# Loading and splitting the first two weight pieces of a stage ahead of its opening

## The chip, the cores and the metric

The kernel runs on one core of one Trainium2 chip. The metric is the device time of one execution in microseconds (us). A core has a matrix engine (TensorE, PE in the profile; its weight loads are PEld), a vector engine (VectorE, DVE), an activation engine (ScalarE, ACT), a general engine (GpSimd, POOL) and a queue engine that issues most transfers (SyncE, SP; SPq in the rows). Engines meet at semaphores only. A block of the program ends in a barrier that all engines must reach.

## The reference, cut to what matters

Five parts follow one another on 512 rows of 1024 numbers, all in float32:

```
h = x
h = layer_norm(alpha*h + window_attention(h))        # layer 0
h = layer_norm(alpha*h + hier_moe(h))                # expert stage 0: 32 experts, each token in 2
h = layer_norm(alpha*h + latent_attention(h))        # layer 1: c = h @ b_w_down, ...
h = layer_norm(alpha*h + hier_moe(h))                # expert stage 1
for l in range(2):                                   # second block
    p = rms_norm(h, norm_mix_pre[l]) @ w_in[l]       # 1024 x 3072, 12 slices of 256 columns
    h = h + rms_norm(mixers(p) @ w_out[l]);  h = h + rms_norm(conv_ffn(rms_norm(h)))
```

`hier_moe` ends in a weighted sum: each token adds the outputs of its two experts, each times its routing weight.

## The kernel before, in words

Rows are worked on in four tiles of 128 rows (`NT` = 4, tile t). The residual stream is `resid`. Products that need float32 accuracy are made from split operands: a value is stored as a high part (rounded, made on ScalarE by `high`) and a low part (value minus high part), and `split_matmul` (L242 to L244) multiplies high by high, high by low and low by high. A weight arrives in pieces of 1 MB, as 128 partitions x 2048 numbers. A piece is loaded into one of two places of `raw`, then `high` (L1646, L2452) and `low` (L1796, L2692) write its parts.

**Expert stage** (`experts`). For each of 32 blocks of 64 slots the weights (6 MB) are streamed in through SP's queue, three sets deep. PE multiplies (L1219, L1237), POOL scatters the results of a block by an indirect DMA into `y_dram` (`r_y`, L1191). SP issues its last weight load long before the last block is done. The stage ends when the last scatter has landed. The tile `hT`, 16 KB in each partition, is not used while this stage runs.

**Opening** of the part behind it (`latent_layer` behind stage 0, `second_block` behind stage 1). It makes the sum of the residual and the experts' rows, a layer norm, in the second block also an RMS norm, a transposition, and a split, tile by tile:

- SP loads `rows[t]` (L499, 1 MB each, from `r_y`), the norm's gain and shift (L428, L429, 0.5 MB each), and the first two weight pieces (L1386, L2047).
- PE: `own` (L512) multiplies `resid` of all four tiles by the identity, into two PSUM banks a tile. `add(t)` (L520) adds the two weighted rows of tile t, and waits for `rows[t]`. After the norm `turn_x(t)` (L1443) or `turn(opening, t)` (L2109) transposes the tile back into the same banks.
- DVE: for tile t `stats` (L446, L448) on PSUM, `centre` (L467), `finish` (L474), and `split_low(t)` (L1787, L2712). In the second block `finish(opening, t)` (L2708) scales by the RMS norm in between.
- ACT: the square root and its companions, `split_high(t)` (L1628, L2474), `high(0)`, `high(1)`.
- POOL makes the low parts of weight pieces 0 and 1 (L1436, L2095). All later low parts are made by DVE.

After the opening PE starts the first product with the first half of the columns (tiles 0 and 1, 256 columns) and does the second half (tiles 2 and 3) when these are there. In the latent layer this is `down_tile(m, columns)` with six output tiles m: before, m = 0 and 1 are done in halves, m = 2 to 5 whole. Each half of a tile is 24 matmuls of 256 columns, a whole one 24 of 512. In the second block it is `in_halves`: four output tiles q of weight pieces 0 and 1, first halves with `turn` calls in between, then the four second halves.

In the latent layer, SP waits until two output tiles are complete (`sp.wait_ge(down, 2)`), since the rotary tables (L1406) and the next weight pieces of `b_w_uq` come after that. ACT makes the high part of that piece (L1644) before it copies output tile 0 out of PSUM (L1651) and squares it (L1655), and PE's `add_squares(0)` (L1459) needs the square.

Between expert stage 1 and the second block stands `sweep`, a block of its own with a barrier on either side, in which POOL, DVE and ACT clear semaphores and SP issues the first loads.

## Time and profile before

| | |
|---|---|
| median of 3 runs | 2841.07 us (2838.81 to 2842.73) |
| profiled execution, device time | 2843.17 us |
| its span in the trace | 2841.4 us |
| TensorE matmul busy | 2533.8 us, 89% |
| VectorE busy | 1078.5 us, 38% |
| ScalarE busy | 776.1 us, 27% |
| GpSimd busy | 179.0 us, 6% |
| opening of the latent layer | from 755.2 us on |
| opening of the second block | from 1570.2 us on |

Times in the rows are microseconds from the start of the span. In a timeline row the first number is the start, the second the time from the start of the first to the end of the last of the x instructions of the row, and in brackets stands how long the engine sat idle before it and what it waited for. The trace shows a float32 matmul of 512 columns as two instructions: `own` and `add` have 16 and 32 rows where the program has 8 and 16 matmuls. PEclk is the granted TensorE clock as a share of full speed: 1.00 is 2.4 GHz and 0.50 is 1.2 GHz.

### The profile page before, as it was taken

To read this page: it belongs to the slowest core of one execution; us is meant where nothing else is said; L and a number is where in the kernel's file an instruction comes from. 1 tells how busy PE (TensorE), PEld (TensorE's weight loads), DVE (VectorE), ACT (ScalarE), POOL (GpSimd) and SP (SyncE) were. 2 spreads that over 40 slices of the span, in tenths; PEclk is the share of its full clock that TensorE was granted. 3 is DMA by queue.
4 is the path that set the end of the run, shared out by engine and by line. 5 is a ranking of instruction groups with operands and counts; after the bars stand their busy time and mean duration, and the time that the engine had idled before them with its cause. 6 is when DMAs were issued, how large, how long until landed. Compare 5 with 4: busy or idle time off the path is not lost. (4 is left out here: it accounts for less than half of the span.)

```text
span 2841.4 us, 36857 instructions
## 1 busy us (share of the span) xinstructions
PE 2533.8 (89%) x14546; PEld 1870.4 (66%) x14546; DVE 1078.5 (38%) x1597; ACT 776.1 (27%) x1234; POOL 179.0 (6%) x284
## 2 busy tenths in 40 slices
PE   8796998887788978997887699999999999999998
PEld 7574555544366665654454487788878876888887
DVE  3653111001244551110000465655551566655632
ACT  3430101000135420100000343543431453544331
POOL 0000111111100001111111100000000000000000
PEclk9996999999998978999999799999999999999999
DMA  5228999999712068999998421313232222232331
GB/s 155 60 79 317 409 407 405 408 409 406 258 71 75 9 260 348 405 406 409 406 413 327 146 97 60 119 60 104 89 120 102 82 71 78 79 100 89 104 119 52
DMA packets 174815, 576.39 MB, mean 203 GB/s; under 512 B 20497, under 2 KB 104017, under 8 KB 125043
## 3 DMA queue, kind: packets, MB, share of 16 engines
q1 hardware_dynamic: 164146, 558.07, 51.7%
q0 software_dynamic: 10560, 16.81, 1.8%
q8 instruction: 77, 1.26, 0.2%
q14 instruction: 32, 0.25, 0.0%
HBM read 569.56 MB, written 23.07 MB: 209 GB/s over the span
## 5 line engine op out<-in xcount | busy, mean ns | idle before, releaser
L1219 PE MATMUL ps<-first_weights,moe_xsT 128*64 128x256 f32 x2688 | 312.3, 381 | 49.9 <-DMA first_weights<-in_moe_w_up 33.1
L242 PE MATMUL ps<-l_h_hi,l_w_hi 128*128 128x512 f32 x896 | 353.0, 394 | 0.0
L244 PE MATMUL ps<-l_h_hi,l_w_lo 128*128 128x512 f32 x896 | 348.8, 389 | 0.0
L243 PE MATMUL ps<-l_h_lo,l_w_hi 128*128 128x512 f32 x896 | 348.8, 389 | 0.0
L1275 DVE TENSOR_TENSOR moe_hid<-moe_silu,ps 128x256 f32<-128x256 f32 x64 | 27.0, 422 | 796.3 <-PE ps L1219 796.3
L1219 PEld LDWEIGHTS ps<-first_weights,moe_xsT 128*64 128x64 f32 x2688 | 223.7, 137 | 148.3 <-issue 98.8
L2692 DVE TENSOR_TENSOR l_w_lo<-l_raw,l_w_hi 128x2048 fp32r<-128x2048 f32 x76 | 174.0, 2292 | 290.7 <-ACT l_w_hi L2452 290.7
L1256 ACT ACTIVATE moe_ys<-ps 128x512 f32<-128x512 f32 x64 | 38.2, 597 | 688.6 <-PE ps L1237 688.6
L1237 PE MATMUL ps<-first_weights,moe_hidT 128*64 128x512 f32 x672 | 177.2, 675 | 38.6 <-DVE moe_hidT L1277 38.6
L2452 ACT ACTIVATE l_w_hi<-l_raw 128x2048 fp32r<-128x2048 f32 x76 | 145.2, 1914 | 187.2 <-PE ps L244 176.3
L1219 PE MATMUL ps<-first_ring,moe_xsT 128*64 128x256 f32 x1408 | 168.5, 388 | 30.7 <-DMA first_ring<-in_moe_w_up 17.1
L242 PEld LDWEIGHTS ps<-l_h_hi,l_w_hi 128*128 128x128 f32 x896 | 168.2, 188 | 37.4 <-issue 2.9
L243 PEld LDWEIGHTS ps<-l_h_lo,l_w_hi 128*128 128x128 f32 x896 | 168.3, 188 | 35.5 <-issue 1.4
L244 PEld LDWEIGHTS ps<-l_h_hi,l_w_lo 128*128 128x128 f32 x896 | 168.2, 188 | 35.5
L1219 PEld LDWEIGHTS ps<-first_ring,moe_xsT 128*64 128x64 f32 x1408 | 119.0, 140 | 84.2 <-issue 58.9
L1237 PEld LDWEIGHTS ps<-first_weights,moe_hidT 128*64 128x64 f32 x672 | 60.0, 152 | 126.8 <-issue 126.8
L1237 PE MATMUL ps<-first_ring,moe_hidT 128*64 128x512 f32 x352 | 87.2, 639 | 20.1 <-DVE moe_hidT L1277 20.1
L1203 PEld LDWEIGHTS ps<-cst,moe_xs 64*128 64x128 f32 x528 | 68.8, 215 | 43.3 <-issue 24.6
L1203 PE MATMUL ps<-cst,moe_xs 64*128 64x64 f32 x528 | 77.9, 289 | 18.1 <-DMA moe_xs<-r_x,moe_take 18.1
L1191 POOL DMA_INDIRECT r_y<-moe_ys,moe_put x64 | 65.6, 1025 | 295.0 <-ACT moe_ys L1256 295.0
L2735 DVE SCALAR_TENSOR_TENSOR l_gate<-l_glu,l_par,l_gate 128x512 f32<-128x512 f32 x120 | 81.0, 744 | 0.1
L242 PE MATMUL ps<-l_w_hi,l_act_hi 128*128 128x512 f32 x192 | 77.0, 401 | 3.6 <-DVE l_conv L2866 3.6
(549 smaller groups left out, 4294.4 us busy)
## 6 DMA issues: line engine op xcount, KB each, us to landing
first_weights<-in_moe_w_up SPq DMA_DIRECT2D x84, 1024.0 KB
first_weights<-in_moe_w_down SPq DMA_DIRECT2D x84, 1024.0 KB
first_weights<-in_moe_w_gate SPq DMA_DIRECT2D x84, 1024.0 KB
first_ring<-in_moe_w_gate SPq DMA_DIRECT2D x44, 1024.0 KB
first_ring<-in_moe_w_up SPq DMA_DIRECT2D x44, 1024.0 KB
first_ring<-in_moe_w_down SPq DMA_DIRECT2D x44, 1024.0 KB
l_raw<-in_ffn_up SPq DMA_DIRECT2D x44, 1024.0 KB, 5.1
l_raw<-in_w_in SPq DMA_DIRECT2D x24, 1024.0 KB, 5.3
```

The lines of the kernel that those rows point to most:

```text
L242: pe.matmul(out, stationary[0], moving[0], start=first, stop=False)
L243: pe.matmul(out, stationary[0], moving[1], start=False, stop=False)
L244: return pe.matmul(out, stationary[1], moving[0], start=False, stop=last)
L1191: pool.indirect_dma_start(out=r.y_dram, out_offset=bass.IndirectOffsetOnAxis(ap=put[:, 0:1], axis=0), in_=ys[:, :], in_offset=None, bounds ...
L1203: ins = pe.transpose(k.ps[:, 0, j * SLOTS:(j + 1) * SLOTS], row_of_tile[:, j // 4, j % 4, :], k.cst[0:SLOTS, C_ID:C_ID + SLOTS])
L1219: ins = pe.matmul(k.ps[64 * h:64 * h + 64, 2 + m, 0:256], xsT[:, j, :], weights.gate_up[s][m][:, j, 256 * h:256 * h + 256], start=j == 0, ...
L1237: ins = pe.matmul(k.ps[64 * h:64 * h + 64, 4, :], hidT[:, j % 2, 64 * (j // 2):64 * (j // 2) + 64], weights.down[s][:, j, 512 * h:512 * h ...
L1256: act.activation(ys[:, :], k.ps[:, 4, :], ACT.Copy).then_inc(ys_kept, 1)
L1275: dve.tensor_tensor(hid[:, :], silu[:, :], k.ps[:, 3, 0:256], ALU.mult).then_inc(hid_kept, 1)
L2452: act.activation(ring[n][0], raw[:, m % 2, :], ACT.Copy).then_inc(hi_made, 1)
L2692: dve.tensor_tensor(lo, raw[:, m % 2, :], hi.bitcast(F32), ALU.subtract).then_inc(lo_made, 1)
L2735: ins = dve.scalar_tensor_tensor(acc, glu[:, i, c:c + SEQ], par[:, l, 2, 2 * c + i:2 * c + i + 1], acc, ALU.mult, ALU.add)
```

## The change

At the end of each expert stage SP issues the first two weight pieces of the part that follows, into `hT` (`k.early`). The opening's ACT and DVE split them first, ahead of the norm's work; POOL no longer does. `own` is called tile by tile between the `add` calls. In the latent layer the first halves of four output tiles, not two, are done before tiles 2 and 3 of the rows are needed. In the second block's `sweep` SP issues only two `rows` loads, PE does `own(0)` there, and the gains, `rows[2]` and `rows[3]` are issued behind the barrier. The order of `split_low`, `stats` and `finish` changes.

```diff
 def sweep(self, loads, products):
+            @block.tensor
+            def _(pe):
+                products(pe)
...
-    def own(self, k, pe):
-        for t in range(NT):
-            for half in range(2):
+    def own(self, k, pe, t):
+        for half in range(2):
...
 def experts(k, layer, r, weights, early):
                 weights.load(sp, layer, LAST_SET, e, free(LAST_SET, q + TURNS))
+            for n in range(2):
+                src, j = early(n)
+                sp.dma_start(k.early[:, n, :].rearrange("p (j c) -> p j c", j=j), src).then_inc(r.early_in, 16)
...
 def latent_layer, SP
-                if p >= 2:
+                if p >= 4:
                     sp.wait_ge(lo_made, done_of(p - 2))
...
-            load(0)
             cl.load(sp, 2)
             cl.load(sp, 3)
-            load(1)
 latent_layer, POOL
-            for p in range(2):
-                pool.wait_ge(hi_made, p + 1)
-                pool.tensor_tensor(whole(p, 1), raw[:, p, :], whole(p, 0).bitcast(F32), ALU.subtract).then_inc(lo_made, 1)
 latent_layer, PE
-            for m in range(2):
-                down_tile(m, slice(2 * P, SEQ)).then_inc(down, 1)
-            for m in range(2, 6):
-                down_tile(m, slice(0, SEQ)).then_inc(down, 1)
-                if m < 5:
+            for m in range(6):
+                down_tile(m, second if m < 4 else slice(0, SEQ)).then_inc(down, 1)
+                if 2 <= m < 5:
                     add_squares(m - 2)
 latent_layer, ACT
-            act.preload_act_table_set("natural_log_exp_and_others")
             cl.diagonals(k, act)
+            high(0)
+            high(1)
+            act.preload_act_table_set("natural_log_exp_and_others")
 latent_layer, DVE
+            low(0)
+            low(1)
             stats(0)
...
             split_low(0)
+            split_low(1)
             stats(2)
             cm.centre(k, dve, 2, tile_banks(2))
-            split_low(1)
...
 second_block, before its block
     def first_loads(sp):
         cl.load(sp, 0)
-        cm.load_gains(k, sp, DEPTH - 1, 1)
-        for t in range(1, NT):
-            cl.load(sp, t)
-    k.sweep(first_loads)
+        cl.load(sp, 1)
+    k.sweep(first_loads, lambda pe: cl.own(k, pe, 0))
 second_block, SP
-            load(0, 0)
-            load(0, 1)
+            cm.load_gains(k, sp, DEPTH - 1, 1)
+            cl.load(sp, 2)
+            cl.load(sp, 3)
 second_block, PE, the turns after first halves 0 to 3
-                in_halves(..., *([((), (2,), (), (3,))] if l == 0 else []))
+                in_halves(..., *([((), (2,), (3,), ())] if l == 0 else []))
```

PE at the opening of the latent layer. The number behind `lat_rows` is a buffer, in the order of tiles 0 to 3. Before:

```order
L512 MATMUL ps<-resid,cst 128x512 x8
L520 MATMUL ps<-lat_rows_3336,lat_diag 128x512 x4
L520 MATMUL ps<-lat_rows_3337,lat_diag 128x512 x4
...
L520 MATMUL ps<-lat_rows_3338,lat_diag 128x512 x4
...
L520 MATMUL ps<-lat_rows_3339,lat_diag 128x512 x4
```

After:

```order
L519 MATMUL ps<-resid,cst 128x512 x4
L527 MATMUL ps<-lat_rows_3338,lat_diag 128x512 x4
L519 MATMUL ps<-resid,cst 128x512 x2
L527 MATMUL ps<-lat_rows_3339,lat_diag 128x512 x4
L1457 MATMUL ps<-cst,resid 128x128 x8
L519 MATMUL ps<-resid,cst 128x512 x2
L527 MATMUL ps<-lat_rows_3340,lat_diag 128x512 x4
L1457 MATMUL ps<-cst,resid 128x128 x8
L527 MATMUL ps<-lat_rows_3341,lat_diag 128x512 x4
```

Four of the eight identity matmuls now stand behind the first `add`, two of them behind the first transposition.

DVE at the opening of the second block, up to the low part of tile 1 (`l_h_lo`, second row). Before:

```order
L446 BN_STATS l_cstats<-ps 128x6 x2
L448 BN_AGGR l_cmv<-l_cstats 128x2
L467 SCALAR_TENSOR_TENSOR resid<-ps,l_cmv,l_cgain 128x1024
L2697 RECIPROCAL l_rs<-l_sd 128x1
L2708 SCALAR_TENSOR_TENSOR l_end_xn_7165<-resid,l_rs,l_end_gain_7162 128x1024
L2884 RECIPROCAL l_crs<-l_clnv 128x1
L474 SCALAR_TENSOR_TENSOR resid<-resid,l_crs,l_cshift 128x1024
L2712 TENSOR_TENSOR l_h_lo<-ps,l_h_hi 128x8x128
L446 BN_STATS l_cstats<-ps 128x6 x2
L448 BN_AGGR l_cmv<-l_cstats 128x2
L467 SCALAR_TENSOR_TENSOR resid<-ps,l_cmv,l_cgain 128x1024
```

After:

```order
L2721 TENSOR_TENSOR l_first_lo<-first_hT,l_first_hi 128x2048 x2
L454 BN_STATS l_cstats<-ps 128x6 x2
L456 BN_AGGR l_cmv<-l_cstats 128x2
...
L482 SCALAR_TENSOR_TENSOR resid<-resid,l_crs,l_cshift 128x1024
L454 BN_STATS l_cstats<-ps 128x6 x2
L456 BN_AGGR l_cmv<-l_cstats 128x2
L475 SCALAR_TENSOR_TENSOR resid<-ps,l_cmv,l_cgain 128x1024
L2741 TENSOR_TENSOR l_h_lo<-ps,l_h_hi 128x8x128
L2726 RECIPROCAL l_rs<-l_sd 128x1
L2737 SCALAR_TENSOR_TENSOR l_end_xn_7215<-resid,l_rs,l_end_gain_7211 128x1024
```

Two low parts of 2048 numbers now stand ahead of the first statistics, and the statistics and centring of tile 2 ahead of the low part of tile 0.

SP around the end of expert stage 1: the two pieces are now the last issues of the stage (`first_hT`), and their old place is gone:

```order
L1175 DMA first_hT<-in_w_in 128x8x256 x2
...
L507 DMA l_rows_7217<-r_y 128x2x1024
L507 DMA l_rows_7218<-r_y 128x2x1024
...
L507 DMA l_rows_7219<-r_y 128x2x1024
L507 DMA l_rows_7220<-r_y 128x2x1024
```

## Rows read from the trace of the kernel before

**Rows 1.** The page, costliest groups: splitting one piece, low and high part.

```profile
L2692 DVE TENSOR_TENSOR l_w_lo<-l_raw,l_w_hi 128x2048 fp32r<-128x2048 f32 x76 | 174.0, 2292 | 290.7 <-ACT l_w_hi L2452 290.7
...
L2452 ACT ACTIVATE l_w_hi<-l_raw 128x2048 fp32r<-128x2048 f32 x76 | 145.2, 1914 | 187.2 <-PE ps L244 176.3
```

**Rows 2.** Busy time by stretch: last blocks of stage 0, openings.

```profile
core 0: us, PE busy (x) PEld busy (x) DVE busy (x) ACT busy (x) POOL busy (x), PEclk, DMA share, GB/s
...
734.00:736.00 2.00, 1.78 (x16) 1.26 (x16) 0.00 (x0) 0.11 (x1) 0.00 (x0) 1.00 0.54 224
...
744.00:746.00 2.00, 1.08 (x6) 0.17 (x2) 0.00 (x0) 0.60 (x1) 0.00 (x0) 1.00 0.00 0
...
1597.00:1608.00 11.00, 1.16 (x9) 0.80 (x7) 8.95 (x8) 4.34 (x6) 4.49 (x1) 0.76 0.00 0
...
1631.00:1637.00 6.00, 5.62 (x27) 5.62 (x28) 4.82 (x3) 2.67 (x2) 0.00 (x0) 0.52 0.01 3
1637.00:1646.00 9.00, 9.00 (x77) 8.85 (x75) 0.00 (x0) 0.09 (x1) 0.25 (x2) 1.00 0.00 0
```

**Rows 3.** Timeline of the latent layer's opening, up to its first products.

```profile
755.21 9.28 PE L512 MATMUL ps<-resid,cst 128*128 128x512 f32 x16 [10.13 <-PEq L1148]
...
767.96 1.30 DVE L446 BATCH_NORM_STATS2 lat_cstats<-ps 128x6 f32<-128x512 f32 x2 [26.38 <-PE ps L520]
...
771.01 1.28 DVE L474 SCALAR_TENSOR_TENSOR resid<-resid,lat_crs,lat_cshift 128x1024 f32<-128x1024 f32 x1
...
782.84 0.39 PE L242 MATMUL ps<-lat_x_hi,lat_d_hi 128*128 128x256 f32 x1 [0.50 <-DVE lat_x_lo L1787]
...
793.90 0.58 PE L242 MATMUL ps<-lat_x_hi,lat_d_hi 128*128 128x256 f32 x1 [2.37 <-DVE lat_x_lo L1787]
```

**Rows 4.** Timeline of the latent layer behind its opening.

```profile
801.35 0.34 SPq L1406 DMA_DIRECT2D lat_tables<-in_k_ropeb  x1
...
806.93 1.57 ACT L1644 ACTIVATE lat_u_hi<-lat_raw 128x1024 fp32r<-128x1024 f32 x2 [11.72 <-DMA lat_raw<-in_b_w_uq]
...
809.53 0.70 PE L1459 MATMUL ps<-lat_sq,cst 128*128 128x512 f32 x1 [2.74 <-ACT lat_sq L1655]
...
832.60 0.50 PE L242 MATMUL ps<-lat_c_q_hi,lat_u_hi 128*128 128x512 f32 x1 [1.22 <-DVE lat_u_lo L1794]
```

**Rows 5.** Timeline of the second block's opening.

```profile
1574.12 2.45 ACT L505 ACTIVATE l_diag<-cst,r_weight 128x128 f32<-128x128 f32 x8 [13.29 <-PEq L189]
...
1583.39 13.90 PE L520 MATMUL ps<-l_rows,l_diag 128*128 128x512 f32 x32
...
1587.02 1.30 DVE L446 BATCH_NORM_STATS2 l_cstats<-ps 128x6 f32<-128x512 f32 x2 [30.39 <-PE ps L520]
...
1594.62 1.29 DVE L2708 SCALAR_TENSOR_TENSOR l_end_xn<-resid,l_rs,l_end_gain 128x1024 f32<-128x1024 f32 x1
...
1602.53 4.49 POOL L2095 TENSOR_TENSOR l_first_lo<-l_raw,l_first_hi 128x2048 fp32r<-128x2048 f32 x1 [28.29 <-ACT l_first_hi L2452]
...
1603.35 4.76 DVE L2708 SCALAR_TENSOR_TENSOR l_end_xn<-resid,l_rs,l_end_gain 128x1024 f32<-128x1024 f32 x1
...
1608.16 1.97 PE L2109 MATMUL ps<-cst,l_end_xn 128*128 128x128 f32 x8 [10.01 <-DVE l_end_xn L2708]
...
1612.50 0.58 PE L242 MATMUL ps<-l_h_hi,l_first_hi 128*128 128x256 f32 x1 [2.37 <-DVE l_h_lo L2712]
...
1646.30 0.50 PE L242 MATMUL ps<-l_h_hi,l_w_hi 128*128 128x512 f32 x1
```

**Rows 6.** DMA issues and time to landing: tiles 0 and 1, scatters.

```profile
lat_rows<-r_y SPq DMA_DIRECT2D x1, 1024.0 KB, 5.2
...
lat_rows<-r_y SPq DMA_DIRECT2D x1, 1024.0 KB, 9.5
...
DMA to landing us min/median/max: 2.6/6.6/13.8
...
746.66 1.02 POOL L1191 DMA_INDIRECT r_y<-moe_ys,moe_put  x1 [4.11 <-ACT moe_ys L1256]
```

More of the change, by code:

```diff
@@ L183, in clear_stale, with early, sweep @@
                 eng.sem_clear(s)
-    def sweep(self, loads):
+    @property
+    def early(self):
+        return self.hT[:, :, :].rearrange("p (n a) s -> p n (a s)", n=2)
+    def sweep(self, loads, products):
         sems = [s for st in self.stale for s in st.sems]
@@ L1127, in for_each_block, with experts @@
         body(LAST_SET, q + TURNS, q + (EXPERTS - 1))
-def experts(k, layer, r, weights):
+def experts(k, layer, r, weights, early):
     st = Stage(k.nc, f"moe{layer}")
@@ L1555, in out_part @@
                     ins.then_inc(am.out_made, 1)
-            cl.own(k, pe)
+            first, second = slice(0, 2 * P), slice(2 * P, SEQ)
+            cl.own(k, pe, 0)
+            cl.own(k, pe, 1)
             cl.add(k, pe, 0)
+            cl.own(k, pe, 2)
             cl.add(k, pe, 1)
             turn_x(0)
+            cl.own(k, pe, 3)
             cl.add(k, pe, 2)
@@ L1639, in high @@
                     act.wait_ge(up, len(kinds))
-                act.wait_ge(loaded[p % 2], 16 * (p // 2 + 1))
-                src = raw[:, p % 2, 0:size(p)]
+                if p < 2:
+                    act.wait_ge(before.early_in, 32)
+                else:
+                    act.wait_ge(loaded[p % 2], 16 * (p // 2))
+                src = source(p)
                 if split(p):
@@ L1790, in low @@
                 dve.wait_ge(hi_made, done_of(p))
-                src = raw[:, p % 2, 0:size(p)]
+                src = source(p)
                 if split(p):
@@ L2024, in second_block @@
     tile_cols = lambda x, t: x[:, :, t * P:(t + 1) * P]
+    piece = lambda m: k.early[:, m, :] if m < 2 else raw[:, m % 2, :]
     unit_bank = lambda u: u if u < 8 else u % 2
@@ L2091, in _ @@
             pool.wait_ge(cleared, 2)
-            for n in range(2):
-                hi, lo = ring[n]
-                pool.wait_ge(hi_made, n + 1)
-                pool.tensor_tensor(lo, raw[:, n, :], hi.bitcast(F32), ALU.subtract).then_inc(lo_made, 1)
             for l in range(DEPTH):
@@ L2403, in turn_parameters @@
                     ins.then_inc(par_turned, 1)
-            cl.own(k, pe)
-            for t in range(NT):
-                cl.add(k, pe, t)
+            cl.own(k, pe, 1)
+            cl.add(k, pe, 0)
+            cl.own(k, pe, 2)
+            cl.add(k, pe, 1)
+            cl.own(k, pe, 3)
+            cl.add(k, pe, 2)
+            cl.add(k, pe, 3)
             turn(opening, 0)
@@ L2450, in high @@
                 m = PIECES * l + n
-                act.wait_ge(loaded[m % 2], 16 * (m // 2 + 1))
-                act.activation(ring[n][0], raw[:, m % 2, :], ACT.Copy).then_inc(hi_made, 1)
+                if m < 2:
+                    act.wait_ge(before.early_in, 32)
+                else:
+                    act.wait_ge(loaded[m % 2], 16 * (m // 2))
+                act.activation(ring[n][0], piece(m), ACT.Copy).then_inc(hi_made, 1)
             def root(g, n, t):
@@ L2653, in _ @@
             cl.diagonals(k, act)
+            high(0, 0)
+            high(0, 1)
             act.wait_ge(cleared, 2)
@@ L2659, in _ @@
             finish(opening, 1, None)
-            high(0, 0)
             deviation(2)
             split_high(opening, 1)
-            high(0, 1)
             finish(opening, 2, None)
             deviation(3)
+            finish(opening, 3, None)
             split_high(opening, 2)
-            finish(opening, 3, None)
             split_high(opening, 3)
@@ L2885, in normed @@
                 cm.finish(k, dve, t)
+            low(0, 0)
+            low(0, 1)
             stats(0)
@@ L2892, in _ @@
             normed(1)
+            stats(2)
             split_low(opening, 0)
-            stats(2)
             finish(opening, 1)
+            normed(2)
             split_low(opening, 1)
-            normed(2)
             stats(3)
             finish(opening, 2)
-            split_low(opening, 2)
             normed(3)
             finish(opening, 3)
+            split_low(opening, 2)
             split_low(opening, 3)
-            dve.wait_ge(lo_made, 2)
             for l in range(DEPTH):
```

38 lines of the change are left out of this document (22 added, 16 removed).

## The prediction

> **What bounds the kernel now.** I read first the busy time by stretch. At full clock PE is busy in every microsecond once a stage runs: 77 matmuls of 256 columns in 9.00 us between 1637 and 1646 [rows 2]. The two openings are where it is not: between 1597 and 1608 PE is busy 1.16 us of 11, and no transfer runs (DMA share 0.00), so DVE (8.95 us) holds it up. Then the timelines, to see which wait ends last. In the latent layer's opening PE spends 9.28 us on `own` alone, adds, and starts its first product at 782.84; it stops again 2.37 us before 793.90, for the low part of tile 3 [rows 3]. In the second block it waits 10.01 us for the scaled tile 1, then 2.37 us, and starts at 1612.50 [rows 5]. What PE loses in an opening the kernel loses, since all behind it hangs on PE's first products. The expert stages are bound by their 1 MB loads, but these are over before the end: the DMA share is 0.54 at 734 to 736 and 0.00 at 744 to 746 [rows 2], and the last scatter is issued at 746.66 [rows 6].
>
> **What is moved, and the price of each part.**
>
> *The early loads* (2 MB a stage) stand behind the last weights in SP's queue. Rows of tile 0 (1 MB) land 5.2 us after issue, tile 1 9.5 us after an issue 1.4 us later, with 1 MB of gains between: 2 MB in some 5.7 us, 2.85 us a MB. Two pieces so take 5.7 us. The last weights run out between 736 and 744; the pieces then end near 745, before the scatter of 746.66. I take 0. Bounds: a scatter takes 2.6 us at best, 6.6 in the median and 13.8 at most [rows 6]; so 0 to 11.2 us a stage, and the value nearest to the stretch with share 0.00 is 0. A gain in the stage itself is excluded, since its own loads are not fewer.
>
> *The split on ACT and DVE*: 2 high parts of 1.91 us, 2 low parts of 2.29 us [rows 1]. ACT starts them after its eight diagonals (2.45 us), DVE ends 2 x 2.29 us after the first high part: 2.45 + 1.91 + 4.58 = 8.9 us after the barrier.
>
> *POOL's two low parts go.* POOL took 4.49 us from 1602.53; the DVE instruction that started at 1603.35 took 4.76 us, where the same instruction took 1.29 us at 1594.62 [rows 5]: it ended 1.1 us after POOL did. These 3.5 us lie inside PE's wait of 10.01 us and go with it.
>
> *Latent layer.* Barrier at 755.2. PE: four instructions for each tile of `own`, eight for each `add`, at 0.43 us each (13.90 us / 32, [rows 5]); the first five come at half clock (9.28 = 5 x 0.85 + 11 x 0.44 and some, [rows 3]). So `own` of tiles 0 and 1 ends at 760.8; rows 0 landed at 760.4. `add(0)` ends at 764.3, and DVE's low parts at 755.2 + 8.9 = 764.1: stats of tile 0 start at 764.4 instead of 767.96. Finish ended 4.33 us after the start of stats (771.01 + 1.28 - 767.96); now at 768.7. Rows 1 land at 766.1 (756.6 + 9.5), just as `own(2)` ends; `add(1)` to 769.6, turn 0 to 770.5 (0.9 each), `own(3)` to 772.3, `add(2)` to 775.8, turn 1 to 776.9, `add(3)` to 780.4. Tile 1: stats from 769.7, finished 774.0, high part after the turn to 778, low part 1.2 us later, 779.2, so hidden. The first product starts at 780.4, 2.4 us earlier. Then PE has four first halves of 2.9 us (24 x 0.12) and two turns, 13.5 us, to 794.0; tile 2 is finished at 783.4 (stats 779.2, + 4.2), just when turn 2 comes; tile 3 at 788.8, its low part at 793.5. The wait of 2.37 us and the half clock behind it go. Output tiles 0 and 1 complete at 794.0 + 2 x 2.9 = 799.8; before it was 801.2, when SP issued the tables (801.35, [rows 4]): 1.4 us earlier.
>
> What is late next is the piece of `b_w_uq`, as before. It landed 5.6 us behind 801.35, at 806.93, and only then did ACT come to the square, which PE got at 809.53, 8.3 us after output tile 1 [rows 4]. That distance stays: now 808.1. But PE has only a half of output tile 2 left to do in it (2.9 us) and waits 5.4 us instead of 2.74. Behind it output tile 3 is a half instead of a whole: 2.9 us instead of the 5.5 that tile 2 took as a whole (from 801.2 to 809.53 - 2.74 = 806.8), 2.6 less. The rest up to 832.60 (squares, root, low parts, PE idle 1.22) hangs on the third square and stays. Gain: 1.4 + 2.6 = **4.0 us**. Half clock behind the wait costs the same as before: it was there too behind 2.74 us.
>
> *Second block.* The barrier of `sweep` stays at 1574.1: SP has three issues less, but `own(0)` in it takes 4 x 0.85 = 3.4 us from 1570.2, to 1573.6. Then `own(1)` 2.0 us; the diagonals are ready at 1576.6, and `add(0)` ends at 1580.1. The remaining two `own` (1.75 each) and three `add` (3.5 each) end at 1594.2; before, 1583.39 + 13.90 = 1597.3. Transfers keep ahead: 2 MB of rows from 1570.2, then gains 1 MB by about 1580.5, rows 2 and 3 by 1583.3 and 1586.2. DVE: low parts until 1574.1 + 8.9 = 1583.0, then stats of tile 0: 1583.1 instead of 1587.02, so the two low parts cost 3 us against `add(0)` and yet leave 3.9 us. The scaled tile 0 came 8.9 us behind the start of stats (1594.62 + 1.29), tile 1's norm 10.3 us; now 1592.0 and 1593.4. Stats and centre of tile 2 to 1596.3 (2.9 us). PE turns tile 0 at 1594.2 to 1595.2, ACT's high part to 1596.3, DVE's low part to 1597.6; ACT squares tile 1 (1.05 + 0.5) to 1597.8; DVE scales tile 1 to 1599.4 instead of 1608.1. Turn 1 to 1600.5, high part (behind ACT's next root) to 1601.6, low part to 1602.9. The first product starts at **1603.0 instead of 1612.5**: 9.5 us.
>
> Then two first halves with half clock at the start (2.9 x 2 + 1.7) to 1610.5; tile 2 was scaled at 1607.3, so turn 2 does not wait; a first half to 1614.3, tile 3 scaled at 1612.0, turn 3, the last first half to 1618.1; tile 3's low part is there at 1617.5. Four second halves (11.5) and the parameters (1.0): 1630.6 where PE was at 1646.30. Of the **15.7 us**, 9.5 are the earlier start, 1.1 + 2.37 two waits that go, 2.4 the half clock behind them (27 matmuls in 5.62 us at clock 0.52, against 0.117 us each, [rows 2]), 0.3 rounding. What follows (tables, pieces 4 on) is issued on PE's progress and moves along.
>
> Sum: 4.0 + 15.7 = 19.7 us. The profiled execution took 2843.17 us, 2.1 above the median; 2843.2 - 19.7 = 2823.5 there, and **2821.4** against the median. Its own range is 2817 to 2826: either opening may be wrong by 2 to 3 us, above all the order of ACT's short waits, and the barrier of `sweep` by 1 us each way.
>
> **Rivals.**
>
> *The latent layer gains nothing.* SP's wait for two complete output tiles comes as late as before: two more first halves (5.8 us) now stand ahead of them, and I leave only 1.4 us of play. If tile 3's low part or turn 2 is late by that, the piece of `b_w_uq` is late and the half tile moved forward is only a longer wait at the square. Then 0 to 1 us there and 15.7 in the second block: 2825. For it: PE's wait at 809.53 exists. Against: PE's chain up to 799.8 has no wait in my table.
>
> *PE stays at half clock in the second block.* It idles 4.3 us behind turn 0 and 2.5 behind turn 1, and the turns are 1 us of work. Before, with idle of 10.0 and 2.37 us, it came back 3.8 us behind 1612.50, and I count the same. If all four first halves go at 0.208 instead of 0.117 us, 96 x 0.09 - 1.7 = 7 us are lost: 2828.5. Against: that start was no better prepared.
>
> *The pieces come late* (the change doesn't do what it says): they would land only behind the barrier, ahead of the rows. Rows then come 5.7 us later in both openings, less the 5.7 us of pieces that no longer stand between: high(0) on both engines waits, and each opening loses about 5: 2832. Against: from 744 to the barrier at 755.2 only the last scatter moves.
>
> *Slower.* The last scatter of each stage, which alone ends it, meets the early pieces. Each would land after up to 13.8 us instead of 2.6 [rows 6]: 2 x 11.2 = 22.4, against 19.7, so 2844. It decides from 9.9 us a stage on. The Trainium skill ("DMA: Bandwidth & Descriptors", section on queues, rings and completion order) has each DMA engine alternate between the queues that have work, whole packets at a time. By this rule a scatter that meets the pieces is held up and not just queued behind them; the rows agree (6.6 us in the median, most of them beside streaming weights, against 2.6 at best).
>
> From the rows alone the milder case of it is 6.6 - 2.6 = 4 us a stage, were the pieces still running at 746.66. Against: share 0.00 at 744 to 746 leaves them room.
>
> **Chances.** Forecast 0.60; latent layer without gain 0.15; half clock 0.08; a scatter held up for 4 us a stage 0.06 (2821.4 + 8 = 2829.4); late pieces 0.04; slower 0.03; 0.04 for more gain than I see (2812 to 2817: the barrier of `sweep` earlier, tile 1 earlier on ACT). The range 2815 to 2830 leaves out about 0.15. No change (within 0.2%, 5.7 us, about what a measurement of this kernel can tell) needs a loss of 14 us against the sum: 0.03. Faster 0.95, slower 0.02.
>
> **What would show it.** In the profile of the changed kernel: the first 256-column product of the latent layer 25.2 us behind the barrier (before 27.6), a wait at the square of about 5 us, PE's first product on `c_q` 73.4 us behind it (before 77.4). In the second block the first product 28.9 us behind `sweep`'s barrier instead of 38.4, no wait between its halves, the 512-column products from 56.5 us on instead of 72.2. The DVE scaling of tile 1 takes 1.3 us. The span of an expert stage is unchanged, and no weight piece is waited for by `high(0)`. I am wrong if the last scatters take over 3 us, if `high(0)` waits for DMA, or if time appears between the openings' ends and the end of the kernel.

## The result, and the profile after

| | median of 4 runs | lowest, highest | ratio to before, 95% interval |
|---|---|---|---|
| before | 2841.28 us | 2838.81, 2842.73 | |
| changed | 2825.61 us | 2823.35, 2828.97 | 0.9946 [0.9931, 0.9962] |

The change gives 15.7 us by the medians. The forecast was 2821.4 us, or 19.7 us less. The measured time lies in its range, 4.2 us above the point. The profiled execution took 2828.97 us with a span of 2827.1: the slowest of the four, so its stages are set beside a second profile of the same kernel below.

The page of the changed kernel, busy times:

```profile
span 2827.1 us, 36949 instructions
...
PE 2532.8 (90%) x14594; PEld 1869.7 (66%) x14594; DVE 1079.9 (38%) x1601; ACT 776.0 (27%) x1234; POOL 159.5 (6%) x280
```

PE does the same work (2533.8 us before). POOL lost 19.5 us. What changed is when PE may start.

The timeline of the latent layer's opening (start, us, engine and line, operation, in brackets the idle time before it and its releaser). The barrier is at 756.6:

```profile
756.66 6.48 PE L519 MATMUL ps<-resid,cst 128*128 128x512 f32 x8 [10.12 <-PEq L1156]
...
760.90 4.49 DVE L1817 TENSOR_TENSOR lat_d_lo<-first_hT,lat_d_hi 128x2048 fp32r<-128x2048 f32 x2 [19.57 <-ACT lat_d_hi L1667]
...
766.61 1.30 DVE L454 BATCH_NORM_STATS2 lat_cstats<-ps 128x6 f32<-128x512 f32 x2 [1.21 <-PE ps L527]
...
781.49 0.68 PE L250 MATMUL ps<-lat_x_hi,lat_d_hi 128*128 128x256 f32 x1
...
801.53 0.34 SPq L1423 DMA_DIRECT2D lat_tables<-in_k_ropeb  x1
...
807.25 1.57 ACT L1665 ACTIVATE lat_u_hi<-lat_raw 128x1024 fp32r<-128x1024 f32 x2 [10.70 <-DMA lat_raw<-in_b_w_uq]
...
809.85 2.07 PE L1473 MATMUL ps<-lat_sq,cst 128*128 128x512 f32 x2 [5.48 <-ACT lat_sq L1676]
...
830.43 0.50 PE L250 MATMUL ps<-lat_c_q_hi,lat_u_hi 128*128 128x512 f32 x1 [1.22 <-DVE lat_u_lo L1815]
```

Against [rows 3, 4], counted from the barrier: statistics after 10.0 us (before 12.75), the first product after 24.9 (27.6; forecast 25.2), the first product on `c_q` after 73.8 (77.4; forecast 73.4). The wait of 2.37 us for the low part of tile 3 is gone. The wait at the square doubled from 2.74 to 5.48 us, as forecast (5.4).

The second block's opening, barrier of `sweep` at 1575.4:

```profile
1575.39 2.44 ACT L513 ACTIVATE l_diag<-cst,r_weight 128x128 f32<-128x128 f32 x8 [13.10 <-PEq L193]
...
1579.67 4.49 DVE L2721 TENSOR_TENSOR l_first_lo<-first_hT,l_first_hi 128x2048 fp32r<-128x2048 f32 x2 [21.57 <-ACT l_first_hi L2481]
...
1584.08 1.29 DVE L454 BATCH_NORM_STATS2 l_cstats<-ps 128x6 f32<-128x512 f32 x2
...
1598.85 1.28 DVE L2737 SCALAR_TENSOR_TENSOR l_end_xn<-resid,l_rs,l_end_gain 128x1024 f32<-128x1024 f32 x1
...
1600.19 1.97 PE L2131 MATMUL ps<-cst,l_end_xn 128*128 128x128 f32 x8 [3.99 <-DVE l_end_xn L2737]
...
1604.53 0.58 PE L250 MATMUL ps<-l_h_hi,l_first_hi 128*128 128x256 f32 x1 [2.37 <-DVE l_h_lo L2741]
...
1632.19 0.50 PE L250 MATMUL ps<-l_h_hi,l_w_hi 128*128 128x512 f32 x1
```

These answer to [rows 5]. The diagonals start at 1575.4 and not at 1574.1, since the stage before ended 1.5 us later; from the barrier on the first product comes after 29.1 us (before 38.4; forecast 28.9) and the 512-column products after 56.8 (72.2; forecast 56.5). The wait of 10.01 us for the scaled tile 1 is now 3.99. DVE's scaling, held up for 3.5 us by POOL, takes 1.28 us again.

Busy time by stretch (the columns are those of [rows 2]): PE in the stretch where it did 1.16 us of 11 before, and in the last 15 us before the 512-column products, where it no longer stops.

```profile
1597.00:1608.00 11.00, 5.44 (x24) 5.04 (x25) 8.79 (x13) 4.42 (x10) 0.00 (x0) 0.57 0.09 30
...
1617.00:1632.00 15.00, 15.00 (x127) 14.75 (x125) 5.72 (x3) 4.83 (x5) 0.25 (x2) 1.00 0.01 1
```

To see where the time went, I cut each profile at the same instructions. *Stage*: first to last scatter of an expert stage. The *tail* is from the last scatter's issue to SP's first issue behind the barrier. *Opening 1*: from there to the first product on `c_q`. *Latent, late*: from SP's issue of the first piece of `b_w_o` to its issue of the gain for the layer norm at the end of the latent layer. *Opening 2*: from SP's first issue in `sweep` to the first 512-column product. The table leaves out three stretches. The one before stage 0 and the one from the first product on `c_q` to the first piece of `b_w_o` differ by under 0.7 us in these five profiles; the one from the end of the latent layer to the first scatter of stage 1 is 189.0 to 191.7 us long. All in us, one profiled execution each:

| kernel | stage 0 | tail | opening 1 | latent, late | stage 1 | tail | opening 2 | opening 2 to end |
|---|---|---|---|---|---|---|---|---|
| before | 468.9 | 8.5 | 77.4 | 45.3 | 469.0 | 8.5 | 76.1 | 1195.1 |
| changed | 470.7 | 8.5 | 73.8 | 46.4 | 470.9 | 8.5 | 60.5 | 1194.9 |
| changed, second profile | 467.9 | 8.5 | 73.6 | 46.4 | 471.7 | 8.5 | 60.1 | 1194.6 |
| opening 1 alone | 467.4 | 8.5 | 74.0 | 46.4 | 471.3 | 8.4 | 76.4 | 1195.0 |
| opening 2 alone | 469.1 | 8.5 | 77.8 | 45.4 | 472.4 | 8.5 | 60.1 | 1192.0 |

Openings gain 3.6 and 15.6 us in the first profile of the changed kernel, 3.8 and 16.0 in the second: 19.2 to 19.8, and 19.7 were forecast. 1.1 us are given back in the late part of the latent layer, in the three profiles here with the new latent opening. The rest of the 4 us lies in expert stages and in the stretch ahead of stage 1, which both vary by 2 us and more between profiles of one kernel. So the questions for the experiments were: does opening 1 deliver, are the scatters held up, and what in the change is it that pays.

### The profile page after: what moved, and what is told of

Read it like the earlier page. It is cut to its first block and busy times, and to the rows that moved or that the text cites. A ratio compares the mean times of both kernels' runs of the same rounds, so it can differ in the third digit from the quotient of the medians.

```text
span 2827.1 us, 36949 instructions
## 1 busy us (share of the span) xinstructions
PE 2532.8 (90%) x14594; PEld 1869.7 (66%) x14594; DVE 1079.9 (38%) x1601; ACT 776.0 (27%) x1234; POOL 159.5 (6%) x280
## 5 line engine op out<-in xcount | busy, mean ns | idle before, releaser
L1248 PE MATMUL ps<-first_weights,moe_hidT 128*64 128x512 f32 x672 | 177.2, 675 | 38.6 <-DVE moe_hidT L1288 38.6
L1248 PEld LDWEIGHTS ps<-first_weights,moe_hidT 128*64 128x64 f32 x672 | 60.1, 152 | 126.8 <-issue 126.8
L1248 PE MATMUL ps<-first_ring,moe_hidT 128*64 128x512 f32 x352 | 88.8, 650 | 20.1 <-DVE moe_hidT L1288 20.1
L1214 PE MATMUL ps<-cst,moe_xs 64*128 64x64 f32 x528 | 77.9, 289 | 19.2 <-DMA moe_xs<-r_x,moe_take 19.2
L1264 ACT ACTIVATE moe_silu<-ps 128x256 f32<-128x256 f32 x64 | 24.5, 383 | 203.2 <-PE ps L1230 203.2
## 6 DMA issues: line engine op xcount, KB each, us to landing
first_weights<-in_moe_w_up SPq DMA_DIRECT2D x84, 1024.0 KB, 29.1
first_weights<-in_moe_w_down SPq DMA_DIRECT2D x84, 1024.0 KB, 28.9
```

The source lines that it names most:

```text
L1214: ins = pe.transpose(k.ps[:, 0, j * SLOTS:(j + 1) * SLOTS], row_of_tile[:, j // 4, j % 4, :], k.cst[0:SLOTS, C_ID:C_ID + SLOTS])
L1248: ins = pe.matmul(k.ps[64 * h:64 * h + 64, 4, :], hidT[:, j % 2, 64 * (j // 2):64 * (j // 2) + 64], weights.down[s][:, j, 512 * h:512 * h ...
```

## Experiments

Opening 1 is that of the latent layer, opening 2 that of the second block. Theory A is the forecast's: both openings gain what was worked out, and nothing is lost outside them. Theory B: the early loads lengthen the stages. Theory C: the latent layer's gain is handed back behind it.

### The same kernel again, opening 1 alone, opening 2 alone

The changed kernel was measured again, beside two kernels that each undo one half of the change. Opening 1 alone:

```diff
     # second block: pieces 0 and 1 from raw again, low parts by POOL, order as before
-            for n in range(2):
+            for n in range(2 if early else 0):
                 src, j = early(n)
-            cl.own(k, pe, 1)
-            cl.add(k, pe, 0)
...
+            for t in range(NT):
+                cl.own(k, pe, t)
+            for t in range(NT):
+                cl.add(k, pe, t)
```

Opening 2 alone undoes the same in the latent layer, with `experts(k, 0, routes[0], weights, None)` and two halves of output tiles instead of four.

> The changed kernel again, for a closer ratio and as the yardstick of the runs beside it. In the profiled execution the two openings gave 3.7 and 15.6 us, while both expert stages were 1.8 us longer and 1.8 us were lost in the latent layer behind its opening. Theory A (chance): the stages and the latent layer wobble by about 2 us from execution to execution, so here these three places come out otherwise: the stages within 1 us of before, the median 15 to 19 us below before. Theory B (contention): the two early pieces hold up the last weights and the last scatter, 1.8 us in each stage in every execution; median 15.5 below. Theory C (given back): what the latent layer's opening gains is lost again before the next expert stage, whatever the run: again 0.3 to 1 us left there.

> Only expert stage 0 loads pieces early, and only the latent layer's opening is changed; stage 1 and the second block are as before. Theory A: 3 to 4 us faster than before. Theory B: 3.7 - 1.8, 2 us faster. Theory C: 0 to 1 us faster.

> Only expert stage 1 loads pieces early, and only the second block's opening is changed. Theory A: 15 to 16 us faster. Theory B: 13.8 us faster, and stage 1 is 1.8 us longer. Theory C says the same as A here. If this alone gives what the whole change gives (15.5), the latent layer's part was worth nothing.

| kernel | median | ratio, interval | gain against 2842.91 |
|---|---|---|---|
| changed | 2826.32 us | 0.9940 [0.9928, 0.9953] | 16.6 |
| opening 1 alone | 2841.68 us | 0.9994 [0.9985, 1.0003] | 1.2, not told from 0 |
| opening 2 alone | 2827.48 us | 0.9943 [0.9930, 0.9956] | 15.4 |

Within the error the second opening is the whole measured gain: 15.4 us where 15.7 were forecast for it. The first one is worth 1.2 us, with an interval from a gain of 4.3 to a loss of 0.9, where 4.0 were forecast. Its own stretch is shorter by 3.4 us in the profile of that very kernel (74.0 against 77.4), so Theory A holds locally. Theory C holds for a part of it: 1.1 us are lost again at one place. PE waits there for the same ScalarE work for the same time. The kernel before, the row and its stretch:

```profile
881.57 0.71 PE L1504 MATMUL ps<-lat_k,lat_q 64*128 64x128 f32 x8 [2.53 <-ACT lat_probs L1691]
...
880.50:887.00 6.50, 4.87 (x30) 3.70 (x30) 1.91 (x7) 2.14 (x9) 0.00 (x0) 0.74 0.00 0
```

The changed kernel in its second profile:

```profile
876.54 1.23 PE L1518 MATMUL ps<-lat_k,lat_q 64*128 64x128 f32 x8 [2.52 <-ACT lat_probs L1712]
...
875.50:882.00 6.50, 5.46 (x30) 4.36 (x30) 1.91 (x7) 1.58 (x7) 0.00 (x0) 0.57 0.00 0
```

The wait is 2.53 and 2.52 us. But behind it the granted clock is 0.74 before and 0.57 now, and the same eight matmuls take 0.71 and 1.23 us. That is a loss the sum had no row for.

It doesn't come with every kernel that has the new opening. The kernel below in which every piece is loaded twice has the same opening, and its late part takes 45.3 us, as before:

```profile
878.03 1.03 PE L1521 MATMUL ps<-lat_k,lat_q 64*128 64x128 f32 x8 [2.53 <-ACT lat_probs L1715]
```

Over all twelve profiles of this document the wait is 2.52 or 2.53 us, and the late part is 45.3 to 45.4 us in four of them and 46.3 to 46.4 us in eight. That the moment at which PE arrives decides between the two is a guess; no run shifts that moment alone.

### The early loads held back until the last weights have landed

```diff
+            wait_then_tick(sp, loaded[LAST_SET][5], n * 16 + TURNS * 16, tick_sp)
-            for n in range(2):
-                src, j = early(n)
+            for p in range(2):
+                src, j = early(p)
...
```

SP waits for the last weights to land before it issues the two pieces.

> The changed kernel, but SP issues the two early pieces only when the last weights of the stage have landed (it waits for the semaphore of the last load), near 740 and 1552. The pieces can then delay no weights, at most the last scatter. Theory A: within 1 us of the changed kernel. Theory B: if the weights were held up, up to 3.6 us faster than it; if it is the scatter, the same or slower, with a last scatter that takes over 3 us to land.

Measured: 2828.95 us, 0.9942 [0.9929, 0.9954], from five executions; a sixth that took 8806 us is left out. That is 2.6 us more than the changed kernel. Its timeline, stage 0 and stage 1:

```profile
743.56 1.02 SPq L1176 DMA_DIRECT2D first_hT<-in_b_w_down  x2
...
749.71 1.02 POOL L1203 DMA_INDIRECT r_y<-moe_ys,moe_put  x1 [5.81 <-ACT moe_ys L1268]
...
759.41 0.37 SPq L507 DMA_DIRECT2D lat_rows<-r_y  x1
...
1562.66 1.02 POOL L1203 DMA_INDIRECT r_y<-moe_ys,moe_put  x1 [4.11 <-ACT moe_ys L1268]
...
1572.98 0.88 SPq L507 DMA_DIRECT2D l_rows<-r_y  x2
```

Nothing moved in the stages: 471.2 and 469.0 us without the pieces beside the weights, against 470.7 and 470.9, 467.9 and 471.7 with them. So Theory B is not borne out in stage 0. Over all twelve profiles stage 0 takes 469.1 us in the median with pieces behind the weights, and 468.9, 469.1 and 471.2 without. Stage 1 takes 471.2 us in the median of nine with them (469.8 to 472.4), and 469.0, 469.0 and 471.3 without: too few to tell. What did move is the tail. The pieces now run beside the last scatter, and from it to the barrier it is 9.7 and 10.3 us instead of 8.5. The trace shows it at the scatter itself: it lands 3.9 and 4.2 us after its issue, against 2.6 or 2.7 us in both stages of the kernel before and of the changed kernel. This is the mechanism of the slower rival, at a price of 1.2 and 1.8 us, not 9.9; together they are about the 2.6 us between the medians.

In the changed kernel SP issues the pieces some 28 us and more ahead of the last scatter (they queue behind the weights), and they are nearly through when it comes. Its timeline and the busy time by stretch in stage 0:

```profile
717.86 20.28 SPq L1175 DMA_DIRECT2D first_hT<-in_b_w_down  x2
...
748.11 1.02 POOL L1202 DMA_INDIRECT r_y<-moe_ys,moe_put  x1 [5.82 <-ACT moe_ys L1267]
```

```profile
740.00:742.00 2.00, 1.09 (x6) 0.48 (x7) 1.02 (x2) 0.00 (x0) 1.06 (x2) 0.96 1.06 360
742.00:744.00 2.00, 2.00 (x7) 0.61 (x5) 0.00 (x0) 0.00 (x0) 0.29 (x2) 0.50 0.50 163
744.00:746.00 2.00, 2.00 (x10) 0.76 (x6) 0.00 (x0) 0.00 (x0) 0.00 (x0) 0.69 0.12 39
```

The last column but one is the DMA share: it falls to 0.12 behind 744. The second piece lands at 747.5, 0.6 us ahead of the scatter's issue at 748.11, where the forecast had it near 745. In stage 1 of the same profile it lands at 1564.3, 1.1 us behind the scatter's issue at 1563.18, and the scatter still takes 2.7 us, with only a small rest left (DMA share 0.07 from 1562 to 1563). So the loads cost nothing, but with little to spare.

The clock of 0.50 and 0.69 beside it can't be put down to the change. In this stage the products of the last block (L1248) took 5.35 us instead of 3.65, and the scatter waited 5.82 us instead of 4.11. The second profile has these 1.7 us at the end of stage 1 and not of stage 0, the kernel with opening 1 alone has them in stage 1, where it loads nothing early, and in the kernel before 9 of the 32 blocks of each stage show such a wait, though neither last one does.

### Every piece loaded twice

```diff
+            for turn in range(2):
+                if turn:
+                    sp.wait_ge(r.early_in, 32)
                 for n in range(2):
```

and the waits for `early_in` in both openings doubled: 4 MB a stage instead of 2.

> The changed kernel, but when the two early pieces have landed SP loads both into the same place once more: 4 MB instead of 2 MB behind the last weights, the second 2 MB from about 746 to 753 and 1559 to 1566, over the last scatter. Where the scatter is held up by running pieces the stage's tail (issue of the last scatter to the barrier, 8.5 us with the pieces done, 9.7 and 10.3 us with the pieces issued late) is 10 to 13 us in both stages: 3 to 9 us more than the changed kernel in all. If a scatter isn't held up, the tail stays at 8.5 us.

Measured: 2829.04 us, 0.9955 [0.9938, 0.9971], where two kernels measured with it took 2824.61 us (`own` in one go) and 2825.50 us (two halves). Stage 1 in its timeline:

```profile
1559.82 0.99 SPq L1178 DMA_DIRECT2D first_hT<-in_w_in  x2
...
1560.27 1.02 POOL L1205 DMA_INDIRECT r_y<-moe_ys,moe_put  x1 [5.81 <-ACT moe_ys L1270]
...
1573.46 0.88 SPq L507 DMA_DIRECT2D l_rows<-r_y  x2
```

The second turn of pieces is issued from 1559.82 on, right with the scatter of 1560.27, and the barrier comes 13.2 us behind it instead of 8.5. The scatter itself lands after 7.1 us instead of 2.7. In stage 0 the second turn is issued at 746.96, 1.1 us behind the scatter of 745.84, which then lands after 3.0 us, and the tail is 8.8 us. So two pieces that meet the last scatter cost up to 4.7 us there. The Trainium skill ("DMA: Bandwidth & Descriptors", section on queues, rings and completion order) has each DMA engine alternate between the queues that have work, a packet at a time. By this rule the scatter is slowed beside the pieces, not queued behind all of them. The trace agrees, without proving the rule: both pieces were issued ahead of the scatter, at 1559.82 and 1560.23, and it landed at 1567.4, while the second piece landed at 1568.3.

### POOL makes the low parts again

```diff
+            for n in range(2):
+                hi, lo = ring[n]
+                pool.wait_ge(hi_made, n + 1)
+                pool.tensor_tensor(lo, piece(n), hi.bitcast(F32), ALU.subtract).then_inc(lo_made, 1)
...
-            low(0, 0)
-            low(0, 1)
             stats(0)
```

The same in the latent layer, where ACT also waits for POOL's two low parts before it splits tile 0: loads early, order new, but DVE no longer makes the two low parts.

> The changed kernel, but GpSimd makes the low parts of pieces 0 and 1 again, from the early pieces, in both openings; ScalarE makes the high parts early, as changed. If the gain is in the earlier order alone, this is no worse than the changed kernel, and 2.9 us a opening better, since VectorE starts its statistics at once (the add of tile 0 ends 1.2 and 2.9 us before VectorE's two low parts do). If what mattered was to keep GpSimd away from VectorE, VectorE's instructions with two SBUF inputs are held again for up to 4.5 us each while GpSimd works (about 762 to 771 and 1580 to 1589), and the openings are 2 to 5 us longer than changed. I expect the latter in the second block, by 2 us, since finish and scale of tile 0 fall into that stretch.

Measured: 2824.85 us, 0.9936 [0.9922, 0.9951]; openings 73.9 and 60.6 us. I had expected a loss of about 2 us, and there is none. Its timeline of the second opening:

```profile
1580.34 9.01 POOL L2124 TENSOR_TENSOR l_first_lo<-first_hT,l_first_hi 128x2048 fp32r<-128x2048 f32 x2 [4.28 <-ACT l_first_hi L2488]
...
1582.40 1.29 DVE L454 BATCH_NORM_STATS2 l_cstats<-ps 128x6 f32<-128x512 f32 x2 [24.06 <-PE ps L527]
...
1586.08 4.35 DVE L482 SCALAR_TENSOR_TENSOR resid<-resid,l_crs,l_cshift 128x1024 f32<-128x1024 f32 x1
```

DVE is again held up: an instruction of 1.28 us takes 4.35, and ends just behind POOL's (1589.35). But its statistics start at 1582.40, as soon as PE is ready, and not at 1584.08 behind its own low parts; counted from SP's first issue that is 1.9 us earlier. So 3.1 us are lost and 1.9 us won, and the opening takes 60.6 us, as it does in the changed kernel (60.5 and 60.1). The Trainium skill ("SBUF — State Buffer", section on the two separate sides) has a VectorE instruction with two inputs in SBUF and a GpSimd instruction that reads SBUF exclude each other for a whole instruction; this row and the 4.76 us of [rows 5] agree. So in the new order it doesn't matter for the time who makes the low parts. POOL's were ready at 1589.35, behind the first statistics, and that was early enough for PE's first product, which came at 1605.17. Before, the first low part was made from 1602.53 on, in the middle of the norm's work. The pieces were there long before that: they landed at 1589.7 and 1592.6, and ACT took them up at 1600.49 and 1611.09. So with the old load place a new order on ACT alone might also have gained something; no run tries it.

### `own` in one go

```diff
             cl.own(k, pe, 1)
-            cl.add(k, pe, 0)
             cl.own(k, pe, 2)
+            cl.own(k, pe, 3)
+            cl.add(k, pe, 0)
             cl.add(k, pe, 1)
```

in both openings, all four `own` ahead of the first `add`.

> The changed kernel, but PE does the identity matmuls of all tiles ahead of the first add again (in the second block tile 0 in the sweep, the other three ahead of the first add). They are the same instructions, so PE's adds end at the same time; the add of tile 0 ends 3.5 us later in the latent layer (768.0 after the barrier times of 756.6: 1.7 + 1.7 us of identity matmuls ahead), VectorE starts its statistics as much later, and the first product comes 1 to 3 us later there. In the second block the low parts hide it: the statistics of tile 0 start at 1584.1 against an add that would end at 1585.0, so under 1.5 us. If the interleaving does nothing, both openings are within 0.5 us of the changed kernel.

Measured: 2824.61 us, 0.9934 [0.9917, 0.9951]; openings 74.2 and 60.8 us, 0.2 to 0.7 us longer each than in the two profiles of the changed kernel. The statistics start later (766.98 in the latent layer, 12.2 us behind the barrier instead of 10.0):

```profile
754.78 8.73 PE L519 MATMUL ps<-resid,cst 128*128 128x512 f32 x16 [10.13 <-PEq L1156]
...
766.98 1.29 DVE L454 BATCH_NORM_STATS2 lat_cstats<-ps 128x6 f32<-128x512 f32 x2 [3.46 <-PE ps L527]
```

Of these 2.2 us nothing reaches the first product, which comes 24.9 us behind the barrier in both kernels; the 1 to 3 us expected there did not come. And 74.2 us lies within what the other profiles with four halves show (72.8 to 74.4). Tile by tile `own` alone is worth nothing that can be told from 0.

### Two halves instead of four in the latent layer

```diff
             down_tile(1, first)
-            down_tile(2, first)
             turn_x(3)
-            down_tile(3, first)
...
-                down_tile(m, second if m < 4 else slice(0, SEQ)).then_inc(down, 1)
+                down_tile(m, second if m < 2 else slice(0, SEQ)).then_inc(down, 1)
```

> The changed kernel, but in the latent layer only output tiles 0 and 1 are done in halves, as before. By the forecast's chain PE then runs out of halves about 5 us before tile 3's low part is there, stops and comes back at half clock, the two complete output tiles come 0.5 to 1.5 us later, and output tile 3 is a whole one behind the square: the products on c_q start 3 to 4 us later than changed, which is nearly the whole 3.7 us that this opening gained. If the gain there came from the early pieces and the earlier start alone, it is within 1 us of the changed kernel.

Measured: 2825.50 us, 0.9936 [0.9919, 0.9953], no different from the changed kernel. Opening 1 is 74.5 us, 0.7 to 0.9 longer, and the late part is 45.3 us again, 1.1 shorter: nearly the same sum. One profile can't tie that late part to the two halves: with four halves and every piece loaded twice it is 74.4 and 45.3 us. Its timeline:

```profile
788.05 1.09 PE L1457 MATMUL ps<-cst,resid 128*128 128x128 f32 x8 [1.13 <-DVE resid L482]
...
791.51 0.58 PE L250 MATMUL ps<-lat_x_hi,lat_d_hi 128*128 128x256 f32 x1 [2.37 <-DVE lat_x_lo L1806]
...
799.98 0.34 SPq L1423 DMA_DIRECT2D lat_tables<-in_k_ropeb  x1
...
808.02 1.13 PE L1473 MATMUL ps<-lat_sq,cst 128*128 128x512 f32 x2 [2.60 <-ACT lat_sq L1674]
...
814.48 1.02 PE L1473 MATMUL ps<-lat_sq,cst 128*128 128x512 f32 x2
```

PE stops again for 2.37 us at 791.51, but SP's tables are issued 45.0 us behind the barrier, and in the changed kernel 44.9: the two more first halves bring the first two output tiles no earlier. From the first square to the next it takes 6.46 us here, 8.01 before (809.53 to 817.54) and 5.54 in the changed kernel (809.85 to 815.39), where half a tile less of work lies between. The waits ahead were 2.60, 2.74 and 5.48 us. The stretch behind each, first before, then with two halves, then the changed kernel:

```profile
809.50:814.50 5.00, 4.97 (x13) 3.65 (x14) 0.86 (x2) 1.55 (x3) 0.00 (x0) 0.66 0.59 210
```

```profile
808.00:813.00 5.00, 4.98 (x20) 3.79 (x21) 0.86 (x2) 1.54 (x3) 0.00 (x0) 1.00 0.58 210
```

```profile
809.80:813.80 4.00, 3.95 (x13) 2.92 (x14) 0.89 (x2) 1.57 (x3) 0.00 (x0) 0.53 0.48 162
```

With two halves the clock stayed full. The same work at the same kind of wait went 1.55 us faster than before, and that pays for most of what the four halves save. In the seven profiles with four halves and the wait of 5.2 to 5.5 us, the step from square to square takes 5.35 to 6.58 us, at a clock of 0.50 to 0.68 over the first 5 us.

### Weight pieces of `b_w_uq` ahead of SP's wait, and a second step

The square's wait of 5.48 us is for the piece of `b_w_uq`, which SP issues only behind two complete output tiles. Two pieces are moved ahead of that wait:

```diff
             load(3)
+            load(4)
+            load(5)
             sp.wait_ge(down, 2)
             sp.dma_start(tables[:, :, :], a["k_ropeb"]).then_inc(tab_in, 16)
-            for p in range(4, O + 4):
+            for p in range(6, O + 4):
```

> The changed kernel, and in the latent layer SP issues the second and third piece of b_w_uq before it waits for two complete output tiles, not behind. The wait of 5.5 us at the first square hangs on the second of these pieces. If that wait is what took the worth of the moved half tile, it goes: ScalarE comes to the square about 2.5 us behind output tile 0, and the latent layer's products on c_q start 5 to 7 us earlier (5.5 us wait and the half clock behind it); median 4 to 6 us below the changed kernel. If something else is as late (the low parts of b_w_uq on VectorE, GpSimd, the root), 0 to 2 us.

Measured: 2815.48 us, 0.9908 [0.9893, 0.9922]. Its timeline:

```profile
769.29 26.31 SPq L1405 DMA_DIRECT2D lat_raw<-in_b_w_uq  x3
...
798.36 0.33 SPq L1425 DMA_DIRECT2D lat_tables<-in_k_ropeb  x1
...
801.04 1.02 PE L1475 MATMUL ps<-lat_sq,cst 128*128 128x512 f32 x2
...
819.82 0.50 PE L250 MATMUL ps<-lat_c_q_hi,lat_u_hi 128*128 128x512 f32 x1 [1.22 <-DVE lat_u_lo L1817]
```

The wait at the square is gone. Opening 1 takes 66.3 us instead of 73.6 to 73.8, so 7.2 to 7.5 us less, where 5 to 7 were expected for it; the stretch from there to the issue of `b_w_o` is 23.9 us as in the changed kernel. The medians give 10.8 us against the changed kernel's 2826.32 and 10.1 against its 2825.61, more than the 4 to 6 expected and some 3 us more than the opening shows. These 3 us can't be placed. This kernel has four halves; with two it was not tried.

The second step takes the same two pieces early and, in the second block, lets ACT and DVE finish tile 1 before they split tile 0:

```diff
             deviation(1)
-            split_high(opening, 0)
             finish(opening, 1, None)
+            split_high(opening, 0)
...
-            stats(2)
+            dve.wait_ge(cl.collected, 3)
+            cm.stats_of_sum(k, dve, 2)
+            finish(opening, 1)
             split_low(opening, 0)
-            finish(opening, 1)
+            cm.centre(k, dve, 2, tile_banks(2))
+            split_low(opening, 1)
             normed(2)
-            split_low(opening, 1)
```

> As the one with b_w_uq first, and in the second block's opening tile 1 is squared before ScalarE makes tile 0's high part, and VectorE scales tile 1 right behind the statistics of tile 2 instead of behind their centring and tile 0's low part. The scaled tile 1 comes about 2.8 us earlier (1597.3 instead of 1600.1 in the times of the changed kernel), and so do turn 1 and the first product: 3 to 4 us less than the one with b_w_uq first alone, if nothing else is as late; below 1 us if PE waits for tile 2 or 3 instead.

Measured: 2812.59 us, 0.9891 [0.9875, 0.9907], the fastest of all. Its wait for the scaled tile 1 fell from 3.99 to 1.24 us:

```profile
1586.18 1.09 PE L2133 MATMUL ps<-cst,l_end_xn 128*128 128x128 f32 x8 [1.24 <-DVE l_end_xn L2739]
...
1589.64 0.58 PE L250 MATMUL ps<-l_h_hi,l_first_hi 128*128 128x256 f32 x1 [2.37 <-DVE l_h_lo L2743]
...
1617.90 0.50 PE L250 MATMUL ps<-l_h_hi,l_w_hi 128*128 128x512 f32 x1
```

Opening 2 starts at 1560.08 here, so it takes 57.8 us, against 60.1 to 61.2 us in the nine other profiles with the new second opening. The first product comes 3.0 us earlier than with the first step alone and the 512-column products 2.4 us earlier; PE still waits 2.37 us for the low part in between. The median is 2.9 us lower, close to the 3 to 4 forecast. The intervals of the two ratios overlap, but each of the four times (2810.40 to 2813.22 us) is below each of the five of the first step (2814.68 to 2820.24 us), so the second step is very likely worth its 2 to 3 us.

## Why the prediction was right, and where it was off

- *Early loads at no cost*: held at the scatter. The tail is 8.4 or 8.5 us in all profiles in which the pieces are issued behind the weights once, as before, and the last scatter of the changed kernel lands after 2.7 us in both stages. The forecast's sign of being wrong was over 3 us. Bounds were 0 to 11.2 us a stage; where the pieces were made to meet the scatter it cost 0.3 to 4.7.
- *Second block, 15.7 us*: held, by 15.6 and 16.0 us in two profiles and 15.4 us by the kernel that has this part alone. The first product came 9.3 us earlier (forecast 9.5). One part of the reasoning was beside the point: who makes the low parts costs nothing in the new order. The new order runs both halves of the split under PE's `own` and `add`. It needs early pieces for that, but how much of the 15.4 us the early load gives and how much the order on ACT and DVE and the shorter `sweep` give is not separated by any run.
- *Latent layer, 4.0 us*: local gain 3.6 and 3.8 us, so the local sum was right. Its first term, 1.4 us, came as 1.2. Its second, **2.6 us for the half of output tile 3**, came as 2.5 in the first profile (8.01 to 5.54 us between the squares), but it is not what the moved halves are worth. Without them the step also shrinks, to 6.46 us, because the clock then stays full. The words on record, "Half clock behind the wait costs the same as before", compared only with the kernel before. With the moved halves the wait is 5.5 us and half clock follows it again: they are worth at most 0.7 to 0.9 us in the opening, by one profile with two halves, and against the slowest opening with four (74.4 us) nothing.
- *Time behind the openings*: the sum had nothing there. 1.1 us are lost at the scores of the latent layer, by the clock, in eight of the ten profiles with the changed latent opening. In sum four halves show no gain over two: 2826.32 and 2825.50 us.
- *The remaining 4 us between 19.7 and 15.7*: 1.1 is the clock at the scores. The other 2 to 3 can't be placed. Medians of the changed kernel were 2825.61 and 2826.32 us, and of its profiles one shows 14.3 us less in the span and the other 19.8. Between profiles the stages, the stretch ahead of stage 1 (189.0 to 191.7 us in the table's five) and the one from opening 2 to the end (1192.0 to 1195.1 us) vary by about what is sought. The forecast's 19.7 us is thus shown for the two openings and not for the whole kernel. A lengthening of stage 1 by 1 to 2 us isn't ruled out.
- *Rivals*: "the latent layer gains nothing" (2825) is nearer to the measured time than the forecast, and opening 1 alone gave 1.2 us, close to its 0 to 1. But its cause is refuted: the rotary tables, and the piece of `b_w_uq` behind them, were issued 44.9 us behind the barrier, 1.2 us earlier than before. PE did not stay at half clock in the second block: the granted clock was 0.50 from 1604 to 1608, 0.90 to 1612 and 1.00 to 1616. The pieces were not late: `high` of both follows the diagonals at 1577.74 without a wait.

## What to carry to other kernels

An opening in which PE waits for the vector engine is shortened by bringing in whatever that engine needs first, into memory that the stage before leaves free, provided that the loads are all but over before the stage's last store; look at the DMA share just ahead of it and at when that store lands. Work that is moved forward in front of a wait need not be a gain: here it lengthened the wait from 2.6 to 5.5 us, and the matrix engine came out of it at about half clock. Look for the transfer that ends the wait, and issue it ahead of the queue's own semaphore wait: here that took 7.2 to 7.5 us off an opening in which two more interleaved half tiles had made no difference to the kernel's time.

## What the runs showed of the hardware

- The same wait of 2.5 us can leave the clock at 0.74 or at 0.57 of full speed over the 6.5 us around it, and eight matmuls at 0.71 or 1.23 us. At another place waits of 2.74 and 2.60 us left it at 0.66 and 1.00. So a change in one place can move 1 to 1.5 us in another; what decides it is not shown.
- A scatter beside 2 MB of loads on another queue landed after 3.0, 3.9, 4.2 and 7.1 us, and after 2.6 or 2.7 us with the loads over or nearly over; the stage's tail grew with it, by 0.3 to 4.7 us.
- A DVE instruction that meets POOL's ends behind it (4.35 us instead of 1.28), and in this kernel it cost nothing that can be measured (openings of 60.6 us with it, 60.5 and 60.1 without).
